# A two-block model on one core: block order of paired products, and the place of GpSimd's subtractions and issues beside them

## Chip, core and metric

The kernel runs on one core of one Trainium2 chip. The metric is the time of one execution on the device in microseconds (us), the median over several runs. Engines: TensorE (PE, with its weight loads PEld), VectorE (DVE), ScalarE (ACT), GpSimd (POOL) and the queue of SyncE (SP).

## What is computed

Two model blocks over 512 positions of width 1024, float32 throughout. The first has two layers: a norm, a wide projection, four kinds of attention (forgetting, top-k, retention, sliding window), gates and merging, an output projection, then a norm and a gated feed-forward of width 2816 with a short convolution. The second (the "tail") adds a modulation, a Fourier and a gated delta mixer, and a feed-forward with a 3x3 convolution. Cut to the lines that the change touches:

```python
for l in range(DEPTH):
    h = rmsnorm(x, attn_norm[l])
    z = h @ w_in[l]                       # tok, kI, qI, kB, q, k, v, gates ...
    ...
    merged = jnp.sum(g * branch, axis=2)
    x = x + merged @ w_out[l]             # "out", 8 products of 128 columns
    h = rmsnorm(x, ffn_norm[l])
    u = causal_dwconv(h @ w_up[l], conv_w[l], conv_b[l])   # "up" f, j
    a, b = jnp.split(u, 2, axis=-1)
    x = x + (jax.nn.silu(a) * b) @ w_down[l]               # "down", 8 products
...
y  = mixer @ w_out                        # tail: "out2"
xl = xl + gt1l * rmsnorm_2(y, g_post_mix) # norm 3
h  = modulate(rmsnorm_2(xl, g_pre_ffn), sh2l, sc2l)        # norm 4, then "up", "down"
```

## The kernel before

**Dense products.** Every projection is cut into products of 128 output columns; a product has 8 blocks (22 for a down product, 4 for a branch), one for each 128 rows of its weights. A block is three matmuls of 128x128 weights over 512 positions (L738 to L740): high part by high part, high by low, low by high, since each operand is held as a rounded part and a rest. Weights come in items of 128x1024 (512 KB, mostly one product), in a fixed stream.

**Where an item goes.** SP loads it into one of 4 raw slots (`load`, L696), as soon as the item four before it has ended on PE (`dense_mark`). GpSimd issues a second copy of it into one of 3 hi slots (`issue(w)`, L2464), which waits until the item three before it has ended. When both have landed, GpSimd subtracts one from the other (`low(w)`, L2474, output `raw_lo`), and PE may open the item (`weights_lo`). GpSimd works in one order written out by hand; an instruction that waits holds all behind it. Its loop over the items of the two layers does `issue(w + 1)`, `low(w)`, then what hangs on item w - 2 (`finished`). Only for `("out", 1)`, and for the second product after a norm, does it take low first.

**Order of the blocks on PE.** `walk` lists the blocks of the products that it is given; for two products it takes a block of each in turn. Such pairs stand where the other operand comes chunk by chunk: tok and kI behind norm (l, 1), up 0,0 and up 0,1 behind norm (l, 2), out 0 and out 1 behind the merging. There PE waits at each k for chunk k's low part, `h_lo`: even chunks from VectorE (L1781, L2105), odd ones from GpSimd (`split_lo_odd`, L2506, and L2532 for the merged sum). Both products of a pair end within a block of each other.

**Norms.** ScalarE squares the 8 chunks, GpSimd adds six times (`add_square`, L2492), PE sums over the rows (`norm_stats`, L860), GpSimd raises to -1/2 (`norm_pow`, L2498), PE spreads the rows (L876), VectorE scales chunk by chunk. ScalarE's square k waits until `square_added` has k - 2 of the sums. Norm X is that of the context (256 positions): its six additions stand behind item `("down", 0)` of layer 1, and PE needs them after product down 0, norm X's rows after product down 1. Norms 3 and 4 lie between out2 and the tail's feed-forward.

**The tail's order on GpSimd** is a straight list: three out2 items ahead, then for products 3 to 7 issue, low and an addition of norm 3; the first two items of up, norm 3, norm 4, `split_lo_odd(4)`; then the loop over up and down. `W_OUT` and `W_UP` are the places of the first out2 and the first up item.

## Time and profile before

| | |
|---|---|
| median of 3 runs | 3184.25 us (3183.17 to 3186.38) |
| the profiled execution | 3182.28 us, its span 3180.5 us |
| TensorE clock granted, mean | 0.973 |
| PE busy | 2976.0 us, 94% of the span, 16704 matmuls |
| GpSimd busy | 1626.1 us, 51% |
| VectorE, ScalarE busy | 1435.0 us, 738.6 us |
| moved by DMA | 491.99 MB, 155 GB/s in the mean |

Times in the trace are microseconds from the span's start. "Idle before" an instruction is the time in which its engine did nothing, and the arrow names what ended it. The granted clock is a share of 2.4 GHz; the clock has two levels, 1.2 and 2.4 GHz. Matmuls overlap, so the pitch from start to start tells what one costs, not its duration.

### The profile page before, as it was taken

Reading aid. Unit: us, or ns where it says so; the run is one execution under the profiler, and the core shown is the slowest. Engines: PE = TensorE matmul, PEld = TensorE weight load, DVE = VectorE, ACT = ScalarE, POOL = GpSimd, SP = SyncE. Lnnn points to the kernel's source line nnn. Section 1 sums busy time; section 2 is a strip of 40 time slices with the busy share of each in tenths; the row PEclk is TensorE's granted clock in tenths of the full one; section 3 lists DMA queues with packets and bytes.
Section 4 is the critical chain, followed back from the end, with each engine's and each line's share of the span. In section 5 each row is a group of like instructions: output and inputs, shape, how many; then the busy total and the mean of one; then the engine's idle time right before and its main releaser. Section 6 shows DMA issues by size and latency. Waiting matters only on the chain.

```text
span 3180.5 us, 41302 instructions
## 1 busy us (share of the span) xinstructions
PE 2976.0 (94%) x16704; PEld 2344.7 (74%) x16704; DVE 1435.0 (45%) x2527; ACT 738.6 (23%) x1585; POOL 1626.1 (51%) x1134
## 2 busy tenths in 40 slices
PE   6999999998999999999999989999899987689998
PEld 4767777777777877677777777777778576578886
DVE  2654443353555027544433525551242377277721
ACT  3334331111121023333322112111132223111110
POOL 5434455556555664344455555545534254456664
PEclk9999999999999999999999999999999999889999
DMA  4433444534666545344444446765433000345554
GB/s 174 168 121 133 146 151 164 174 124 164 231 225 236 187 158 171 130 137 146 141 152 165 153 145 227 248 224 175 169 119 133 14 3 22 99 139 192 192 198 139
DMA packets 133565, 491.99 MB, mean 155 GB/s; under 512 B 14832, under 2 KB 14832, under 8 KB 132608
## 3 DMA queue, kind: packets, MB, share of 16 engines
q1 hardware_dynamic: 70736, 260.86, 25.1%
q0 software_dynamic: 61200, 222.85, 19.5%
q10 hardware_dynamic: 1440, 5.64, 0.5%
q8 instruction: 133, 2.18, 0.3%
q14 instruction: 56, 0.46, 0.1%
HBM read 487.17 MB, written 2.13 MB: 154 GB/s over the span
## 4 chain that ended last, share of the span: by engine, by line
PE 77%; DVE 9%; POOL 6%; issue 5%; DMA 2%; ACT 1%; POOLq 0%; DVEq 0%; ACTq 0%
PE dense L738 21%; PE dense L740 20%; PE dense L739 20%; POOL raw_lo L2474 3%; PE scores L942 2%; PE O L976 2%; PE turned L964 1%; DMA weights_hi<-stream 1%; POOL squares_sum L2492 1%; PE scores L738 1%; PE scores L740 1%; PE scores L739 1%; PE O L1010 1%; DVE row_sum L1957 1%; PE dense L1134 1%
## 5 line engine op out<-in xcount | busy, mean ns | idle before, releaser
L2474 POOL TENSOR_TENSOR raw_lo<-raw,weights_hi 128x1024 fp32r<-128x1024 f32 x425 | 1021.9, 2405 | 101.5 <-DMA weights_hi<-stream 55.8
L738 PE MATMUL dense<-h_hi,weights_hi 128*128 128x512 f32 x2208 | 891.6, 404 | 32.6 <-POOL raw_lo L2474 17.1
L740 PE MATMUL dense<-h_hi,raw_lo 128*128 128x512 f32 x2208 | 868.6, 393 | 0.0
L739 PE MATMUL dense<-h_lo,weights_hi 128*128 128x512 f32 x2208 | 868.2, 393 | 0.0
L2464 POOL DMA_DIRECT2D weights_hi<-stream x425 | 245.0, 576 | 1184.9 <-PE dense L740 1052.2
L738 PEld LDWEIGHTS dense<-h_hi,weights_hi 128*128 128x128 f32 x2208 | 420.0, 190 | 161.5 <-issue 69.3
L740 PEld LDWEIGHTS dense<-h_hi,raw_lo 128*128 128x128 f32 x2208 | 419.1, 190 | 91.3
L739 PEld LDWEIGHTS dense<-h_lo,weights_hi 128*128 128x128 f32 x2208 | 420.3, 190 | 81.3
L738 PE MATMUL dense<-hidden_hi,weights_hi 128*128 128x512 f32 x528 | 207.0, 392 | 6.3 <-POOL raw_lo L2474 6.3
L739 PE MATMUL dense<-hidden_lo,weights_hi 128*128 128x512 f32 x528 | 206.0, 390 | 0.0
L740 PE MATMUL dense<-hidden_hi,raw_lo 128*128 128x512 f32 x528 | 205.9, 390 | 0.0
L2082 DVE SCALAR_TENSOR_TENSOR x<-dense,x 128x512 f32<-128x512 f32 x32 | 22.1, 692 | 304.7 <-PE dense L740 304.7
L2440 DVE SCALAR_TENSOR_TENSOR side_b<-scores,small_sb,side_b 128x441 f32<-128x441 f32 (+2 forms) x176 | 122.4, 695 | 43.5 <-ACT side_b L1740 38.0
L2119 DVE SCALAR_TENSOR_TENSOR side_b<-dense,small_sb,side_b 128x511 f32<-128x511 f32 x88 | 65.9, 749 | 163.5 <-ACT side_b L1581 162.0
L738 PEld LDWEIGHTS dense<-hidden_hi,weights_hi 128*128 128x128 f32 x528 | 99.5, 188 | 28.6 <-POOL raw_lo L2474 7.1
L1393 ACT ACTIVATE swapped<-dense 32x512 f32<-32x512 f32 x168 | 98.9, 589 | 90.7 <-PE dense L740 76.1
L1895 DVE TENSOR_TENSOR y_parts<-O,y_parts 128x512 fp32r<-128x512 f32 x24 | 16.6, 692 | 218.6 <-ACT y_parts L1474 218.6
L740 PEld LDWEIGHTS dense<-hidden_hi,raw_lo 128*128 128x128 f32 x528 | 99.5, 188 | 20.7
L739 PEld LDWEIGHTS dense<-hidden_lo,weights_hi 128*128 128x128 f32 x528 | 99.6, 189 | 20.5
L1966 DVE TENSOR_SCALAR probs<-probs,inv_sum 128x128 f32<-128x128 f32 (+2 forms) x192 | 111.8, 624 | 3.4
L1500 ACT ACTIVATE probs<-probs,neg_max 128x128 f32<-128x128 f32 (+3 forms) x128 | 71.0, 555 | 176.1 <-DVE neg_max L1939 176.1
L1365 ACT ACTIVATE squares<-x 128x512 f32<-128x512 f32 x56 | 34.8, 629 | 316.0 <-DVE x L2082 282.0
(374 smaller groups left out, 4487.3 us busy)
## 6 DMA issues: line engine op xcount, KB each, us to landing
raw<-stream SPq DMA_DIRECT2D x473, 512.0 KB, 3.5
weights_hi<-stream POOLq DMA_DIRECT2D x425, 512.0 KB, 4.6
decays<-stream ACTq DMA_DIRECT2D x8, 512.0 KB, 3.9
gates<-f_scratch SPq DMA_DIRECT2D x2, 1536.0 KB, 8.6
x<-x_in SPq DMA_DIRECT2D x2, 1024.0 KB, 8.2
dft<-dft SPq DMA_DIRECT2D x4, 512.0 KB, 6.7
out<-x SPq DMA_DIRECT2D x4, 512.0 KB, 2.6
const<-consts ACTq DMA_DIRECT2D x1, 1024.0 KB, 10.7
```

The lines of the kernel that those rows point to most:

```text
L738: nc.tensor.matmul(to, wh, xh, start=first, stop=False)
L739: nc.tensor.matmul(to, wh, xl, start=False, stop=False)
L740: return nc.tensor.matmul(to, wl, xh, start=False, stop=final)
L942: last = nc.tensor.matmul(scores[:, hh, 0:n], qT[c % 2][half, s * P:(s + 1) * P], keys[half, k0:k1], start=True, stop=True)
L976: last = nc.tensor.matmul(O[half, m * P:m * P + n], values[:, m, v0:v0 + HEAD_DIM], probT(hh, m, n), start=(m == 0), stop=True, skip_group ...
L1393: last = nc.scalar.activation(swapped[32 * q:32 * q + 32, :], src[32 * (q ^ 1):32 * (q ^ 1) + 32, :], ACT.Copy)
L1500: last = nc.scalar.activation(prob(s, hh, n), src, ACT.Exp, bias=neg_max[:, at:at + 1], scale=QK_SCALE if name == "D" else 1.0, accum_out= ...
L1966: last = nc.vector.tensor_scalar(prob(s, hh, n), prob(s, hh, n), inv_sum[:, at:at + 1], None, ALU.mult)
L2119: nc.vector.scalar_tensor_tensor(out=u, in0=src[:, 0:SEQ - shift], scalar=small[:, at + tap:at + tap + 1], in1=u, op0=ALU.mult, op1=ALU.ad ...
L2440: nc.vector.scalar_tensor_tensor(out=u, in0=v, scalar=small[:, tap:tap + 1], in1=u, op0=ALU.mult, op1=ALU.add).then_inc(conv_step if m < 7 ...
L2464: nc.gpsimd.dma_start(w_hi(s), stream[DENSE.items[DENSE.weight_list[w]]]).then_inc(hi_landed[s], 16)
L2474: nc.gpsimd.tensor_tensor(lo, src, hi, ALU.subtract).then_inc(weights_lo, 1)
```

## The change

Two orders of blocks are added. With `AFTER_NORM` a pair goes in turns through chunks 0 to 3, then the first product takes chunks 4 to 7 and then the second. It holds for tok with kI and for the up pair of the two layers, not for the tail's. With `AFTER_MERGE` out 0 takes chunks 0 to 5, out 1 chunks 0 and 1, out 0 its last two, out 1 the rest. The number of blocks, items and matmuls is the same, and so is the order in which items are opened.

On GpSimd, low(w) comes ahead of issue(w + 1) for `("qI", 0)` and `("up", 1, 0)`, the first items behind such pairs. Norm X's six additions are cut into three behind item down 1 and three behind down 2. In the tail, issue runs one item further ahead of low in out2, the last addition of norm 3 follows low(W_UP), and low(W_UP + 2) comes ahead of issue(W_UP + 3).

```diff
--- before.py
+++ after.py
@@ -129,6 +129,8 @@
 Block = namedtuple("Block", "key k n out item m opens last mark")
 
 
+AFTER_NORM = [(j, k) for k in range(4) for j in range(2)] + [(j, k) for j in range(2) for k in range(4, KC)]
+AFTER_MERGE = ([(0, k) for k in range(6)] + [(1, 0), (1, 1), (0, 6), (0, 7)] + [(1, k) for k in range(2, KC)])
 EARLY = [("ab", 1), ("qkv", 0, 1), ("qkv", 1, 1)]
 
 
@@ -138,26 +140,26 @@
     def __init__(self):
         rows, items, uses = [], [], {}
 
-        def walk(l, *prods):
+        def walk(l, *prods, order=None):
             n = [n_blocks(p) for p in prods]
-            for k in range(max(n)):
-                for p, total in zip(prods, n):
-                    if k < total:
-                        kind = p[0]
-                        if kind == "wb":
-                            item, m = (l, "wb", p[1], p[2] // 2), (p[2] % 2) * PAIRS + k
-                        elif kind == "down":
-                            item, m = (l, "down", (p[1] * FC + k) // KC), (p[1] * FC + k) % KC
-                        elif kind in ("qkv", "ab"):
-                            item, m = (l,) + p[:-1], k
-                        elif kind in ("wf", "pc", "py"):
-                            item, m = None, 0
-                        else:
-                            item, m = (l,) + p, k
-                        rows.append(((l,) + p, k, total, item, m))
+            for j, k in order or [(j, k) for k in range(max(n)) for j in range(len(prods))]:
+                p, total = prods[j], n[j]
+                if k < total:
+                    kind = p[0]
+                    if kind == "wb":
+                        item, m = (l, "wb", p[1], p[2] // 2), (p[2] % 2) * PAIRS + k
+                    elif kind == "down":
+                        item, m = (l, "down", (p[1] * FC + k) // KC), (p[1] * FC + k) % KC
+                    elif kind in ("qkv", "ab"):
+                        item, m = (l,) + p[:-1], k
+                    elif kind in ("wf", "pc", "py"):
+                        item, m = None, 0
+                    else:
+                        item, m = (l,) + p, k
+                    rows.append(((l,) + p, k, total, item, m))
 
         for l in range(DEPTH):
-            walk(l, ("tok",), ("kI",))
+            walk(l, ("tok",), ("kI",), order=AFTER_NORM)
             for p in [("qI", 0), ("qI", 1), ("kB",)] + lead("A", 0):
                 walk(l, p)
             for t in range(NT):
@@ -165,7 +167,7 @@
                     walk(l, p)
             for d in range(KC):
                 walk(l, ("wb", "C", d))
-            walk(l, ("out", 0), ("out", 1))
+            walk(l, ("out", 0), ("out", 1), order=AFTER_MERGE)
             for d in range(2, KC):
                 walk(l, ("out", d))
             self.ffn(walk, l)
@@ -220,7 +222,7 @@
     @staticmethod
     def ffn(walk, l):
         first = int(l == TAIL)
-        walk(l, ("up", 0, first), ("up", 0, 1 - first))
+        walk(l, ("up", 0, first), ("up", 0, 1 - first), order=AFTER_NORM if l < TAIL else None)
         ada = [("ada", q, k) for q in range(ADA_Q) for k in range(KC)] if l < TAIL else []
         for f in range(1, FC):
             for j in (first, 1 - first):
@@ -2565,6 +2567,9 @@
                     norm_pow(name)
                     issue(w + 1)
                     split_lo_odd(name)
+                elif what in (("qI", 0), ("up", 1, 0)):
+                    low(w)
+                    issue(w + 1)
                 else:
                     issue(w + 1)
                     low(w)
@@ -2575,8 +2580,8 @@
                     group_pow(l, PAIRS - 2)
                 if what == ("gate", "C", KC - 1):
                     group_pow(l, PAIRS - 1)
-                if item == (DEPTH - 1, "down", 0):
-                    for step in range(1, KC - 1):
+                if item in ((DEPTH - 1, "down", 1), (DEPTH - 1, "down", 2)):
+                    for step in range(3 * what[1] - 2, 3 * what[1] + 1):
                         add_square("X", step, CTX)
                 if item == (DEPTH - 1, "down", 4):
                     norm_pow("X", CTX)
@@ -2676,14 +2681,14 @@
                 nc.gpsimd.tensor_tensor(y_lo[:, g, :], yT[:, g, :], y_hi_t[:, g, :], ALU.subtract).then_inc(four_lo, 1)
             pool.wait_ge(p_dve, P_MEANS)
             nc.gpsimd.tensor_tensor(oscale[:], osum[:], minus_half[:, 0:TB * GH], ALU.pow).then_inc(l2_ready, 1)
+            issue(W_OUT + 3)
             for d in range(3, KC):
-                issue(W_OUT + d)
+                issue(W_OUT + d + 1)
                 low(W_OUT + d)
                 add_square(3, d - 2)
-            issue(W_UP)
-            add_square(3, KC - 2)
             issue(W_UP + 1)
             low(W_UP)
+            add_square(3, KC - 2)
             norm_pow(3)
             low(W_UP + 1)
             for step in range(1, KC - 1):
@@ -2691,9 +2696,12 @@
             issue(W_UP + 2)
             norm_pow(4)
             split_lo_odd(4)
+            low(W_UP + 2)
+            issue(W_UP + 3)
             for w in range(W_UP + 2, len(DENSE.weight_list)):
-                issue(w + 1)
-                low(w)
+                if w > W_UP + 2:
+                    issue(w + 1)
+                    low(w)
                 what = DENSE.weight_list[w][1:]
                 if what[0] == "up" and what[1] >= 2 and what[2]:
                     hidden_low(what[1] - 2)
```

## Rows read from the trace of the kernel before

**Rows 1.** The page, part 1: each engine's busy time, share of the span, instructions.

```profile
PE 2976.0 (94%) x16704; PEld 2344.7 (74%) x16704; DVE 1435.0 (45%) x2527; ACT 738.6 (23%) x1585; POOL 1626.1 (51%) x1134
```

**Rows 2.** Waits of PE, whole span: us in total, times, longest us.

```profile
PE dense L738 <- POOL raw_lo L2474: 30.6, 11, 6.3
...
PE dense L738 <- issue: 5.3, 2, 2.7
```

**Rows 3.** Windows of PE, out stage, layer 0: us, busy (x), clock, DMA share, GB/s.

```profile
698.37:713.90 15.53, 12.86 (x49) 0.89 0.20 68
716.77:723.90 7.13, 7.13 (x24) 0.76 0.51 190
723.90:729.35 5.45, 5.45 (x26) 1.00 0.60 192
```

**Rows 4.** One line's instructions: L2474 (ns min/median/max), L2464 (landing).

```profile
L2474 POOL TENSOR_TENSOR raw_lo<-raw,weights_hi x425: 463/2402/2912, 28.0 to 3149.9; 128x1024 fp32r<-128x1024 f32 x141, 128x128 fp32r<-128x128 f32 x1
...
DMA to landing us min/median/max: 3.5/4.6/9.4
```

**Rows 5.** Timeline of GpSimd, up pair, layer 0: start us, us, instruction [idle before].

```profile
765.54 1.29 POOL L2506 TENSOR_TENSOR h_lo<-h,h_hi 128x512 fp32r<-128x512 f32 x1 [0.76 <-ACT h_hi L1384]
772.68 0.57 POOL L2464 DMA_DIRECT2D weights_hi<-stream  x1 [5.85 <-PE dense L740]
773.28 2.37 POOL L2474 TENSOR_TENSOR raw_lo<-raw,weights_hi 128x1024 fp32r<-128x1024 f32 x1
...
778.20 2.91 POOL L2474 TENSOR_TENSOR raw_lo<-raw,weights_hi 128x1024 fp32r<-128x1024 f32 x1 [2.04 <-DMA weights_hi<-stream]
```

**Rows 6.** Timeline of PE, end of the same pair and the next item.

```profile
772.22 0.39 PE L738 MATMUL dense<-h_hi,weights_hi 128*128 128x512 f32 x1
...
776.56 0.39 PE L738 MATMUL dense<-h_hi,weights_hi 128*128 128x512 f32 x1
```

**Rows 7.** Timeline of GpSimd, tok and kI, layer 0.

```profile
39.37 1.29 POOL L2506 TENSOR_TENSOR h_lo<-h,h_hi 128x512 fp32r<-128x512 f32 x1 [0.76 <-ACT h_hi L1384]
...
46.67 2.35 POOL L2474 TENSOR_TENSOR raw_lo<-raw,weights_hi 128x1024 fp32r<-128x1024 f32 x1
```

**Rows 8.** Timeline of GpSimd and VectorE, out pair, layer 0.

```profile
699.06 2.81 POOL L2474 TENSOR_TENSOR raw_lo<-raw,weights_hi 128x1024 fp32r<-128x1024 f32 x1
...
703.17 1.27 POOL L2532 TENSOR_TENSOR h_lo<-merged,h_hi 128x512 fp32r<-128x512 f32 x1 [0.80 <-ACT h_hi L1571]
...
714.27 2.36 POOL L2474 TENSOR_TENSOR raw_lo<-raw,weights_hi 128x1024 fp32r<-128x1024 f32 x1
...
702.34 0.68 DVE L2105 TENSOR_TENSOR h_lo<-merged,h_hi 128x512 fp32r<-128x512 f32 x1
```

**Rows 9.** Timeline of GpSimd, squares of norm X and down 1, layer 1.

```profile
2149.79 4.54 POOL L2492 TENSOR_TENSOR squares_sum<-squares_sum,squares 128x256 f32<-128x256 f32 x5 [0.53 <-ACT squares L1365]
...
2154.87 2.35 POOL L2474 TENSOR_TENSOR raw_lo<-raw,weights_hi 128x1024 fp32r<-128x1024 f32 x1
```

**Rows 10.** Windows of PE: down 0, blocks 8 to 11; out2, products 5 to 7.

```profile
2150.86:2161.67 10.81, 4.55 (x13) 0.68 0.49 147
2741.36:2767.12 25.76, 20.33 (x73) 0.87 0.46 143
```

**Rows 11.** Timeline of GpSimd, out2, product 5.

```profile
2736.53 0.58 POOL L2464 DMA_DIRECT2D weights_hi<-stream  x1
2741.55 2.33 POOL L2474 TENSOR_TENSOR raw_lo<-raw,weights_hi 128x1024 fp32r<-128x1024 f32 x1 [4.44 <-DMA weights_hi<-stream]
```

**Rows 12.** Timeline of GpSimd, up pair of the tail.

```profile
2807.38 1.29 POOL L2506 TENSOR_TENSOR h_lo<-h,h_hi 128x512 fp32r<-128x512 f32 x1 [1.55 <-ACT h_hi L1384]
2810.70 0.61 POOL L2464 DMA_DIRECT2D weights_hi<-stream  x1 [2.04 <-PE scores L740]
2811.34 2.36 POOL L2474 TENSOR_TENSOR raw_lo<-raw,weights_hi 128x1024 fp32r<-128x1024 f32 x1
...
2816.55 2.39 POOL L2474 TENSOR_TENSOR raw_lo<-raw,weights_hi 128x1024 fp32r<-128x1024 f32 x1 [2.36 <-DMA weights_hi<-stream]
```

## The prediction

> **What bounds the kernel now.** The page comes first: TensorE is busy 94% of the span [rows 1]. So the question is never whether GpSimd or the queues are busy (POOL stands at 51%), only where TensorE stands still. The list of PE's waits answers it: the dense products waited 30.6 us, 11 times, for GpSimd's subtraction that makes `raw_lo` of a weight item, and 5.3 us in two gaps that the profile calls "issue" [rows 2]. In the timeline all of these but two short ones lie at places that the diff touches. A window of steady work gives the yardstick: one item (8 blocks of three matmuls) takes PE 5.45 us at full clock, 0.68 us a block [rows 3]. Beside it an item costs GpSimd 0.57 us to issue and about 2.40 us to subtract; a transfer issued by GpSimd lands 3.5 to 9.4 us later, 4.6 at the median [rows 4]. With three hi slots, an item's transfer can start only when the item three before it has ended.
>
> **The pairs after a norm (tok with kI, up 0 with up 1, two layers each).** In the up pair of layer 0 GpSimd ends its last `h_lo` at 766.83, then sits 5.85 us in front of issue(up 1,1), which waits for the first of the pair; both end within one block of each other, at about 772.4 and 773.1. Only then comes low(up 1,0), 773.28 to 775.65 [rows 5]. PE's last block of the pair starts at 772.22 and the second block of the next item at 776.56: 4.34 us for two blocks that need 1.36, so 2.98 us lost [rows 6]. The same subtraction after tok and kI starts at 46.67 [rows 7], again right behind an issue, and costs 2.96 by the same reckoning.
>
> After the change low goes first. It can run from 766.85 to 769.2, under the pair's last blocks; its gap goes whole. The price to look for is chunks: order AFTER_NORM wants chunk 7 at block 11 of the pair and not at 14. Blocks 0 to 7 are unchanged, so block 11 starts at about 769.5, and the last `h_lo` ends at 766.83 [rows 5]: 2.6 us to spare, no cost. In tok and kI block 11 stands at 42.9 against 40.66 [rows 7].
>
> What is next late is low of the item after that. Its transfer can be issued 2.04 us (three blocks) earlier, at about 770.64, since the first product ends three blocks earlier. In the old run it took from 772.68 to 778.20 with two raw loads beside it, 5.5 us, and its subtraction 2.91 [rows 5]. With one raw load beside it at first, the median 4.6 [rows 4] is nearer. PE wants that item at 772.9 + 5.45 = 778.35. By 4.6 and 2.4 us it is ready at 777.6: no wait. By 5.5 and 2.9 it is ready at 779.05: 0.7 us of wait. So between 0 and 0.7 us a site; I take 0.2, nearer to the quiet case. Four sites: 2 x 2.96 + 2 x 2.98 - 0.8 = **11.1 us**.
>
> The Trainium skill (DMA: Bandwidth & Descriptors, Anatomy of one DMA) fits a GpSimd-issued transfer by 2.0 us plus its bytes at 436 GB/s: by estimate 3.2 us for 512 KB alone, 4.4 with one of the same size beside it, 5.6 with two. The trace agrees (3.5 least, 4.6 median, 5.5 here), and by that page the wait would be nearer to none.
>
> **The out pair.** Here two gaps go. The window from out 0's first block to the pair's end takes 15.53 us, 16 blocks need 10.90: 4.63 lost [rows 3], of which 2.67 is PE in front of out 1's first block until low(out 1) ends at 701.87 [rows 8], the rest the clock, granted at 0.89 over the window (its levels are 1.2 and 2.4 GHz). From 713.90 to 716.77 PE stands behind low(out 2), 714.27 to 716.63, which again sits behind an issue [rows 8]: 2.87. The item then takes 7.13 instead of 5.45, at a clock of 0.76: 1.68 [rows 3]. Together 9.18; layer 1 repeats it with 9.21.
>
> With AFTER_MERGE out 1's first block comes sixth, at 698.37 + 6 x 0.68 = 702.45, when `raw_lo` is ready (701.87). Chunk 6 is wanted at 703.8; VectorE writes it until 703.02. Chunk 7 is wanted at 704.5 and GpSimd ends it at 704.44 [rows 8]: no margin, so I charge 0.1 us. Out 0 then ends at 705.2, issue(out 3) and low(out 2) follow at 705.7 and 706.3 to 708.7, and the pair ends at 709.3. PE never stops, and so I expect the clock to stay at 2.4 GHz: both falls followed a gap of 2.7 us. Gain 18.4 - 0.2 = **18.2 us**.
>
> **The squares of norm X.** Behind low(down 0) GpSimd adds six squares, the last five from 2149.79 to 2154.33, and only then issues and makes low(down 1), 2154.87 to 2157.22 [rows 9]. PE wanted it at 2150.86; by the window the next four blocks took until 2161.67, 10.81 us for 2.72, at 0.68 of the clock [rows 10]: 8.1 lost. After the change low(down 1) comes first, ready at about 2148.1; three additions end at 2151.7, low(down 2) runs to 2154.7 (wanted at 2156.3), three more additions end near 2157.4. PE needs the whole sum at the end of product down 0, 2160.4: 3 us to spare. Gain **8.1 us**.
>
> **out2 in the tail.** The loop issues an item and subtracts it at once, so the landing is never hidden: issue at 2736.53, `raw_lo` from 2741.55 [rows 11]. GpSimd's round is then some 8 us against PE's 5.45, and PE, one item after another, loses its lead. From the start of product 5 to the end of product 7 it takes 25.76 us at 0.87 of the clock, where three items need 16.35 [rows 10]: 9.4 lost. With issue(d + 1) in front of low(d), transfer and subtraction of an item have two items of PE's time (10.9 us) for 0.6 + 4.6 + 2.4. The first of them, low(3), moves behind a wait for product 1 (until 2725.5) and ends at 2728.5, wanted at 2730.5. Square 6 of norm 3 is now added behind low of the next stage, at 2757.0; PE wants the sum at 2757.7. Cover 0.7 us; without it each us is lost whole. Gain **9.4 us**.
>
> **The tail's up pair.** Block order is unchanged there. low(W_UP + 2) can start at 2808.66 instead of 2811.34 [rows 12], so the 2.76 us gap before that item nearly closes. But the item after it is issued behind this subtraction at 2811.1, not at 2810.70; it landed 5.85 us later, and its subtraction ended at 2818.95, just when PE wanted it [rows 12]. So PE starts it no sooner: the gap moves one item on. Now four transfers start within 1.3 us instead of three, so it may land 0 to 1.2 us later again; with the 0.4 of the issue that is 0.1 to 1.6 us lost, and 0.6 is what I take. No gain here: **0.6 us slower**. By the page's fit, four 512 KB transfers at once would take 6.8 us, and the loss would be 1.3.
>
> **The sum.** 11.1 + 18.2 + 8.1 + 9.4 - 0.6 = 46.2 us. About 13 of them are clock. The profiled execution took 3182.28 us (span 3180.5) and would take 3136.1; the median of the runs shown lies 1.97 above it, so 3184.25 - 46.2 = 3138.0. PE hands time gained in one stage to the next: the other stages start from PE's own products, and its other waits (norms, VectorE's top-k, the scan) lie after them in order.
>
> **Rivals.**
> (a) The gap moves instead of going. What I find in the tail happens also at the four pairs after norms, because the transfer of the second next item is late. For it: a wait of 2.04 us for its landing in rows 5. Against: it starts 2 us earlier now. Nothing of the 11.1 would be left: 3149. Chance 0.12.
> (b) The merge order bites, or the clock. Chunk 7 has no margin; a late `h_lo` of 1.3 us and a fall of the clock (1.7) in both layers cost 6 us; a few new falls elsewhere cost the same. 3145. Chance 0.12.
> (c) Slower. Moving low in front of issue leaves GpSimd one transfer behind, and the backlog does not heal. Each such item costs what out2 shows, (25.76 - 16.35) / 3 = 3.1 us; from 15 such items on the gain is eaten, and 30 give 3184 - 46 + 93 = 3231. Against: a round of GpSimd's is 3.0 to 4.3 us against 5.45, so it gains over 1 us an item. Chance 0.03.
> (d) The change doesn't do what it says: the subtractions were waiting for something else, their landing for instance, and the same end is kept. 3184. Against: no low at these places shows such a wait but the second one. Chance 0.03.
> More gain than in my forecast (fewer clock falls elsewhere, 3130) has 0.04; the forecast, 3132 to 3144, has 0.66.
>
> A measurement of this kernel can tell some 0.2% (6.4 us) from no change. Faster by more: 0.66 + 0.12 + 0.12 + 0.04 = 0.94; same 0.03; slower 0.03. The range of 8 in 10 takes in (a) and (b) and their ends: 3129 to 3153.
>
> **What would show it.** Right: PE's wait for `raw_lo` on the dense lines falls from 30.6 to under 6 us; the 2.7 us gaps after tok/kI, out, up are gone; the clock stays full over the out pairs; out2 runs at 5.45 us an item. In the tail the gap of 2.8 us stands one item later. Wrong: waits for DMA in front of low of the second next item over 0.7 us at the pairs, new waits for `h_lo` at blocks 8 to 11, or a wait of norm 3's sum at PE.

## The result, and the profile of the changed kernel

The changed kernel took 3138.98 us (median of 4 runs, 3135.69 to 3141.66) beside 3184.68 us for the kernel before on the same chip: ratio 0.9857, 95% interval 0.9844 to 0.9869. That is 45.7 us less, where 46.2 had been forecast. Measured once more with the last experiments it took 3136.56 us against 3186.22 (ratio 0.9852, 0.9836 to 0.9869). The profiled execution took 3141.11 us with a span of 3139.3, so 41.2 us less than the span before. Line numbers of the kernel have moved by two: L738 is now L740, L2464 is L2466, L2474 is L2476.

The page's part 1, beside [rows 1]: TensorE's busy time fell by 12 us, since less of it runs at 1.2 GHz; the rest of the gain is time in which it no longer stands.

```profile
PE 2963.7 (94%) x16704; PEld 2338.8 (75%) x16704; DVE 1448.9 (46%) x2527; ACT 738.4 (24%) x1585; POOL 1625.7 (52%) x1134
```

The waits of PE over the whole span (us in total, times, longest us), beside [rows 2]: the wait of the dense line for `raw_lo` fell from 30.6 us in 11 places to 8.2 in 3, and the row "issue" of 5.3 us is gone. The tail's gap of 2.8 us isn't in the 30.6: before the change it stood in a row of its own, the second below, since that product writes to another tile.

```profile
PE dense L740 <- POOL raw_lo L2476: 8.2, 3, 3.5
...
PE scores L738 <- POOL raw_lo L2474: 2.8, 1, 2.8
```

The windows of PE in the changed kernel (us, busy, matmuls, clock, DMA share, GB/s) answer to [rows 3] and [rows 10]. In order: the out pair of layer 0, the product behind it, blocks 3 to 11 of down 0 in layer 1, and out2 from the last block of product 4 to that of product 7. Busy time equals the window in each, and the clock is full.

```profile
695.63:706.66 11.03, 11.03 (x49) 1.00 0.57 183
706.66:712.10 5.44, 5.44 (x25) 1.00 0.59 206
2118.31:2124.57 6.26, 6.26 (x29) 1.00 0.73 255
2705.44:2721.76 16.32, 16.32 (x73) 1.00 0.57 194
```

GpSimd's timeline of the up pair in layer 0 (start, duration, instruction, idle time before it), beside [rows 5]: the subtraction of up 1,0 now stands directly behind the last `h_lo`, the two issues come 2.7 us apart as the two products end, and the subtraction of up 1,1 ends at 765.47. PE wanted it at 765.5.

```profile
752.82 1.30 POOL L2508 TENSOR_TENSOR h_lo<-h,h_hi 128x512 fp32r<-128x512 f32 x1 [0.76 <-ACT h_hi L1386]
754.08 2.40 POOL L2476 TENSOR_TENSOR raw_lo<-raw,weights_hi 128x1024 fp32r<-128x1024 f32 x1
757.75 0.57 POOL L2466 DMA_DIRECT2D weights_hi<-stream  x1 [1.28 <-PE dense L742]
760.47 0.53 POOL L2466 DMA_DIRECT2D weights_hi<-stream  x1 [2.15 <-PE dense L742]
762.56 2.91 POOL L2476 TENSOR_TENSOR raw_lo<-raw,weights_hi 128x1024 fp32r<-128x1024 f32 x1 [1.56 <-DMA weights_hi<-stream]
```

The same for the out pair of layer 0, beside [rows 8]: `raw_lo` of out 1 is ready at 699.16 and wanted at 699.7; the `h_lo` of chunk 7 ends at 701.75, where PE wants it at 701.85; the subtraction of out 2 ends at 706.04, 0.6 us ahead of its product.

```profile
696.32 2.84 POOL L2476 TENSOR_TENSOR raw_lo<-raw,weights_hi 128x1024 fp32r<-128x1024 f32 x1
...
700.47 1.28 POOL L2534 TENSOR_TENSOR h_lo<-merged,h_hi 128x512 fp32r<-128x512 f32 x1 [0.79 <-ACT h_hi L1573]
703.05 0.57 POOL L2466 DMA_DIRECT2D weights_hi<-stream  x1 [1.30 <-PE dense L742]
703.64 2.40 POOL L2476 TENSOR_TENSOR raw_lo<-raw,weights_hi 128x1024 fp32r<-128x1024 f32 x1
```

In the tail's up pair, beside [rows 12], both issues follow the first subtraction as one entry (x2), and the transfer of the first of them landed at 2772.94, 6.73 us after its issue.

```profile
2763.52 2.40 POOL L2476 TENSOR_TENSOR raw_lo<-raw,weights_hi 128x1024 fp32r<-128x1024 f32 x1
2766.21 1.21 POOL L2466 DMA_DIRECT2D weights_hi<-stream  x2 [0.29 <-PE scores L742]
2773.08 2.33 POOL L2476 TENSOR_TENSOR raw_lo<-raw,weights_hi 128x1024 fp32r<-128x1024 f32 x1 [5.66 <-DMA weights_hi<-stream]
```

To see where the 41.2 us of the span came from, the start of the last block of every product was compared in the two traces; a step in that difference belongs to the place where it occurs.

| place | forecast us | step in the traces us |
|---|---|---|
| four pairs after norms | 11.1 | 2.97 + 2.94 + 3.00 + 2.85 = 11.8 |
| out pair, two layers | 18.2 | 9.13 + 8.89 = 18.0 |
| squares of norm X | 8.1 | 8.1 |
| out2 | 9.4 | 9.4 |
| tail's up pair | -0.6 | -2.6 |
| three norms ahead of pairs, clock | none | +3.3 |
| turn A 3, layer 1 | none | -3.5 |
| qkv 2 in the tail | none | -2.9 |
| all the rest | none | -0.4 |

The parts named in the forecast give 44.7 us of the 46.2. Below it stand gains and losses at places that the change doesn't touch, and the experiments show that these come and go from one kernel to the next.

### The profile page after: what moved, and what is told of

Its sections match the earlier page's. It is cut to its first block, busy times and chain, and to the rows that moved or that the text cites. A ratio compares the mean times of both kernels' runs of the same rounds, so it can differ in the third digit from the quotient of the medians.

```text
span 3139.3 us, 41302 instructions
## 1 busy us (share of the span) xinstructions
PE 2963.7 (94%) x16704; PEld 2338.8 (75%) x16704; DVE 1448.9 (46%) x2527; ACT 738.4 (24%) x1585; POOL 1625.7 (52%) x1134
## 4 chain that ended last, share of the span: by engine, by line
PE 82%; DVE 7%; POOL 5%; issue 3%; DMA 2%; ACT 1%; POOLq 0%; DVEq 0%; ACTq 0%
PE dense L740 22%; PE dense L742 21%; PE dense L741 21%; POOL raw_lo L2476 2%; PE scores L944 2%; PE O L978 2%; PE turned L966 1%; POOL squares_sum L2494 1%; PE scores L740 1%; PE scores L741 1%; PE scores L742 1%; DMA weights_hi<-stream 1%; PE O L1012 1%; DVE row_sum L1959 1%; PE dense L1136 1%
## 5 line engine op out<-in xcount | busy, mean ns | idle before, releaser
L2476 POOL TENSOR_TENSOR raw_lo<-raw,weights_hi 128x1024 fp32r<-128x1024 f32 x425 | 1021.9, 2405 | 81.6 <-DMA raw<-stream 38.9
L740 PE MATMUL dense<-h_hi,weights_hi 128*128 128x512 f32 x2208 | 890.3, 403 | 14.8 <-DVE h_lo L1783 10.2
L2466 POOL DMA_DIRECT2D weights_hi<-stream x425 | 244.8, 576 | 1169.1 <-PE dense L742 1058.6
L740 PEld LDWEIGHTS dense<-h_hi,weights_hi 128*128 128x128 f32 x2208 | 418.8, 190 | 141.7 <-issue 55.4
L740 PE MATMUL dense<-hidden_hi,weights_hi 128*128 128x512 f32 x528 | 206.2, 390 | 0.0
L740 PEld LDWEIGHTS dense<-hidden_hi,weights_hi 128*128 128x128 f32 x528 | 99.1, 188 | 21.6 <-issue 0.9
L740 PE MATMUL dense<-y_parts,weights_hi 128*128 128x512 f32 x256 | 103.5, 404 | 2.8 <-DVE y_parts L2008 2.8
## 6 DMA issues: line engine op xcount, KB each, us to landing
const<-consts ACTq DMA_DIRECT2D x1, 1024.0 KB, 10.8
```

The lines of the kernel that those rows point to most:

```text
L740: nc.tensor.matmul(to, wh, xh, start=first, stop=False)
L2466: nc.gpsimd.dma_start(w_hi(s), stream[DENSE.items[DENSE.weight_list[w]]]).then_inc(hi_landed[s], 16)
L2476: nc.gpsimd.tensor_tensor(lo, src, hi, ALU.subtract).then_inc(weights_lo, 1)
```

## The experiments

All ratios are against the kernel before, run on the same chip between them. "Stretch" is the time in the profiled execution from the first block of a place to the last block that its gaps can reach.

### The out order alone, whole and half

```
+AFTER_MERGE = ([(0, k) for k in range(6)] + [(1, 0), (1, 1), (0, 6), (0, 7)] + [(1, k) for k in range(2, KC)])
-            walk(l, ("out", 0), ("out", 1))
+            walk(l, ("out", 0), ("out", 1), order=AFTER_MERGE)
```

> The kernel before with one part of the change: the block order AFTER_MERGE for the out pair of both layers. Theory: both gaps of the pair are the place of the first product's end and of the second product's first block, so the order alone brings 9.1 us a layer, as in the kernel after: 18.3 us in all, 3166 us, and the trace shows neither the 2.7 us wait in front of out 1's first block nor the 2.8 us wait in front of out 2. Rival: the pair waits for GpSimd's h_lo of chunk 7 (no margin) or the time comes back in the up stage: 3172 us or more. Rival: nothing but the whole change together works: 3184 us.

Measured: 3164.29 us against 3184.18, ratio 0.9939 (0.9917 to 0.9962), so 19.4 us less (12 to 26). The stretch from out 0's first block to out 3's fell from 25.53 us (both windows of [rows 3] and the gap between them) to 16.48, by 9.05 us, in layer 1 from 25.56 to 16.55. No GpSimd line was edited: the end of the first product alone moves the issue and the subtraction behind it.

For the half, the second line of the order reads:

```
+AFTER_MERGE = ([(0, k) for k in range(6)] + [(1, k) for k in range(6)] + [(0, 6), (1, 6), (0, 7), (1, 7)])
```

> The kernel before with half of AFTER_MERGE: out 1 opens sixth, but out 0 ends at block 14 and out 1 at block 15, as before. Theory: the first gap goes (2.67 us and the clock fall behind it, 4.6 us a layer), the second one in front of out 2 stays, with its own fall of the clock (2.87 + 1.68 us a layer): 9.2 us gained, 3175 us. Rival A: the clock fell for another reason than the gap, so the first half gives only 2 x 2.67 = 5.3 us: 3179 us. Rival B: the time not lost in the first gap is lost in the second, which ends at the same moment: 3184 us.

Measured: ratio 0.9966 (0.9953 to 0.9980), 10.8 us less (6 to 15). The windows of the same stretch in this kernel, layers 0 and 1:

```profile
695.95:715.33 19.38, 16.66 (x73) 1.00 0.48 162
1812.87:1833.90 21.03, 18.30 (x74) 0.92 0.45 151
```

In both, span less busy is 2.7 us: the second gap stands as before. Rival B falls, the two gaps are independent; rival A's 5.3 us lies outside the interval too, narrowly. But the clock fell behind the remaining gap in layer 1 and not in layer 0, with the same gap and the same work. So the clock's part, priced at 3.6 us a layer, is not a fixed price of the gaps.

### TensorE kept at work in the gaps

```
                         if e.item[0] < TAIL and e.item[1:] in (("out", 1), ("out", 2)):
                             pe.wait_ge(t_copied, T_LAYER * (e.item[0] + 1))
                             for _ in range(11):
                                 nc.tensor.matmul(turned[:, 0, :], h_hi_t[:, 0, 0:P], h_hi_t[:, 0, :], start=True,
                                                  stop=True, skip_group_check=True)
                         pe.wait_ge(weights_lo, DENSE.weights[e.item] + 1)
```

> The kernel before, where TensorE works in the two gaps of each out pair: 11 matmuls of 128x512 into a bank that nobody reads, ahead of the wait for raw_lo of out 1 and of out 2 (some 2.4 of the 2.7 and 2.9 us). The waits stay as long as they are. Theory: the clock falls behind a gap because PE stood still; with the gaps filled it stays at 2.4 GHz over the out pairs, and 1.96 + 1.68 us a layer come back, 7.3 us: 3177 us. Rival: the clock falls at this place whether PE stands still or not: 3184 us. Rival: the filling matmuls end after raw_lo is ready and delay the product by more than the clock gives back: over 3184 us.

Measured: ratio 0.9989 (0.9978 to 1.0000), 3.5 us less (0 to 7). The windows of the stretch, layers 0 and 1, have the clock at 1.00:

```profile
700.96:724.20 23.24, 22.12 (x96) 1.00 0.39 135
1819.91:1843.10 23.19, 22.06 (x95) 1.00 0.40 137
```

The clock stayed full in all four filled gaps, and 2.3 and 2.4 us of 25.5 came back, where 3.6 had been forecast. Most of the missing part is the filling itself: out 1 opened at 705.53, 1.0 us after its `raw_lo` was ready at 704.50. How much this shows is limited by the kernels that leave the gaps empty. There are ten such stretches (the kernel before and the four experiments that don't touch the out order, two layers each), and three of them kept the clock too, at 22.3 us:

```profile
1826.34:1848.65 22.31, 16.91 (x74) 1.00 0.40 142
```

(the experiment with out2 alone, layer 1). By these a kept clock is worth 3.2 us a layer and not 3.6. The other seven stretches lie at 23.6 to 26.8 us with a clock of 0.81 to 0.93. Counted by single gaps, those of the halved pair included, a fall stood behind 13 of 22 empty gaps and behind none of the four filled ones. So an empty gap of 2.7 us made a fall of the clock likely at this place and not certain. That standing still is the cause is supported by the two filled stretches and by every stretch without a gap at 1.00; it isn't proved by two.

### The norm order alone, and GpSimd's order alone

```
+AFTER_NORM = [(j, k) for k in range(4) for j in range(2)] + [(j, k) for j in range(2) for k in range(4, KC)]
-            walk(l, ("tok",), ("kI",))
+            walk(l, ("tok",), ("kI",), order=AFTER_NORM)
-        walk(l, ("up", 0, first), ("up", 0, 1 - first))
+        walk(l, ("up", 0, first), ("up", 0, 1 - first), order=AFTER_NORM if l < TAIL else None)
```

> The kernel before with the block order AFTER_NORM in tok with kI and up 0 with up 1 of both layers; GpSimd's order of issue and low is as before. Theory: the first product ends 3 blocks (2.04 us) earlier, issue and the low behind it go with it, and the gap of 2.97 us in front of the next item shrinks to about 0.9 us at each of the four places: 8.2 us gained, 3176 us. Rival: the gap is set by the landing, which does not come earlier: 3184 us.

Measured: ratio 0.9971 (0.9958 to 0.9984), 9.2 us less (5 to 13). The steps at the four places are 1.99, 2.02, 2.04 and 2.05 us, as the three blocks (2.04 us) of the theory.

The other half leaves the block order and puts low first:

```
+                elif what in (("qI", 0), ("up", 1, 0)):
+                    low(w)
+                    issue(w + 1)
```

> The kernel before with only GpSimd's order changed at the items behind the pairs after norms: low first, then issue; the block order is as before. Theory: the gap in front of the next item goes at all four places, but the item after it is issued at the old time while TensorE wants it 2.97 us earlier, so a gap of 2.5 to 2.9 us stands one item later, as in the tail of the kernel after: 0 to 1.9 us gained, and up to 3 us lost where its transfer is slow, 3182 to 3187 us. Rival: the landing has reserve, and moving low alone brings the whole 11.9 us: 3172 us.

Measured: ratio 0.9999 (0.9988 to 1.0010): nothing. The rival, 11.9 us, lies outside. GpSimd's timeline of the up pair in layer 0 shows why:

```profile
769.28 1.21 POOL L2464 DMA_DIRECT2D weights_hi<-stream  x2 [3.60 <-PE dense L740]
776.83 2.34 POOL L2474 TENSOR_TENSOR raw_lo<-raw,weights_hi 128x1024 fp32r<-128x1024 f32 x1 [6.34 <-DMA weights_hi<-stream]
```

Both products end within one block, both issues go out together behind them, and the first transfer lands after 7.41 us (6.61 and 5.58 us behind tok and kI of layers 0 and 1, 5.52 behind up of layer 1). PE stands 2.07 us in front of up 1,1 and 2.83 in front of qI 1 (0.62 and 1.82 in layer 1). That is rival (a) of the prediction, to be seen wherever only half of the change is made. There is a second wait that neither theory had, in PE's list of waits:

```profile
PE dense L738 <- DVE side_a L2119: 3.7, 2, 1.9
```

Up 1,0 writes into the bank of up 0,0, and VectorE still reads that bank with its convolution until 771.4. In the kernel before this wait lay hidden under the wait for `raw_lo`; in the changed kernel the first product ends three blocks earlier and the bank is free in time (this row of PE's is in neither of the two traces). So AFTER_NORM serves two ends, the slot for the next transfer and the bank, and GpSimd's order is worth something only with it: 8.1 of the 11.8 us come with the block order, and the remaining 3.7 with both.

### The squares of norm X alone, out2 alone

```
-                if item == (DEPTH - 1, "down", 0):
-                    for step in range(1, KC - 1):
+                if item in ((DEPTH - 1, "down", 1), (DEPTH - 1, "down", 2)):
+                    for step in range(3 * what[1] - 2, 3 * what[1] + 1):
```

> The kernel before with only the squares of norm X moved: three behind low(down 1), three behind low(down 2). Theory: PE's 2.1 us-and-clock loss at product down 0 goes whole, 8.0 us of PE's time between the last up block and the end of down 0, and nothing comes back since the sum is needed 3 us after its end: 3176 us. Rival: the additions now delay low(down 3) or the norm, and half comes back: 3180 us.

Measured: ratio 0.9973 (0.9963 to 0.9984), 8.6 us less (5 to 12); the step at down 0 is 8.11 us. The window from its first block to block 12 was 16.39 us at a clock of 0.79 before, and is now

```profile
2144.74:2153.03 8.29, 8.29 (x40) 1.00 0.72 253
```

For out2, the loop of the tail as in the change, without the part for the up pair:

```
+            issue(W_OUT + 3)
             for d in range(3, KC):
-                issue(W_OUT + d)
+                issue(W_OUT + d + 1)
                 low(W_OUT + d)
                 add_square(3, d - 2)
-            issue(W_UP)
-            add_square(3, KC - 2)
             issue(W_UP + 1)
             low(W_UP)
+            add_square(3, KC - 2)
             norm_pow(3)
```

> The kernel before with only the loop of out2 changed: each item issued one round ahead, the last square of norm 3 behind low of the up stage. Theory: products 5 to 7 run at 5.45 us each instead of 25.76 us for the three, 9.4 us gained, 3175 us, and the tail's up pair stays as before with its gap of 2.8 us. Rival: the late square holds the norm at PE (0.7 us of cover) and takes back 1 to 3 us: 3177 us.

Measured: ratio 0.9973 (0.9960 to 0.9986), 8.6 us less (4 to 13). From the start of product 5 to the last block of product 7 it was 22.41 us at 0.85, and is now

```profile
2745.40:2761.04 15.64, 15.64 (x71) 1.00 0.57 202
```

The whole step in the traces is 9.4 us, and no wait for the sum of norm 3 took it back. Added up, the parts measured alone (19.4, 9.2 and 0.3 for the two halves of the norm pairs, 8.6, 8.6) give 46.1 us; the whole, in two measurements, 45.7 and 49.7. Each part is known to some 4 to 7 us only, so this sum tells that no large part is missing, and the steps in the traces tell the parts.

### The tail's up pair undone

```
-            low(W_UP + 2)
-            issue(W_UP + 3)
             for w in range(W_UP + 2, len(DENSE.weight_list)):
-                if w > W_UP + 2:
-                    issue(w + 1)
-                    low(w)
+                issue(w + 1)
+                low(w)
```

> The changed kernel with GpSimd's order in the tail's up pair as it was before: issue(W_UP + 3), then low(W_UP + 2). Theory: the change only moved the gap one item on and made the transfer slower, so undoing it brings a gap of 2.8 us in front of up 1,1, none in front of up 1,0, and 2.0 to 2.6 us less in all: 3136.5 us against 3139. Rival: the transfer of up 1,0 takes 6.7 us for another reason, the gap of 3.5 us stays and that of 2.8 us comes on top: 3142 us.

Beside it ran the changed kernel once more:

> The changed kernel as it is, beside the three that follow. All theories: 3139 us, with VectorE's negation of row_max taking 2.7 to 2.9 us in the last turn of branch A (0.17 us elsewhere) in one or both layers.

Measured: 3136.81 us against 3136.56 for the changed kernel beside it (ratios 0.9850 and 0.9852, intervals of 0.003): the two can't be told apart by their times, and the 2.0 to 2.6 us forecast are not seen there. (In the changed kernel's second profile the negation took 2.85 and 2.91 us, held in both layers.) The traces can. From the first block of the pair to the last of up 1,0 it took 26.31 us in the kernel before, 29.31 and 29.01 in the two profiles of the changed kernel, 27.45 with this part undone. GpSimd in this kernel:

```profile
2762.47 0.61 POOL L2466 DMA_DIRECT2D weights_hi<-stream  x1 [1.50 <-PE scores L742]
2763.11 2.36 POOL L2476 TENSOR_TENSOR raw_lo<-raw,weights_hi 128x1024 fp32r<-128x1024 f32 x1
2765.41 0.57 POOL L2466 DMA_DIRECT2D weights_hi<-stream  x1
2769.70 2.81 POOL L2476 TENSOR_TENSOR raw_lo<-raw,weights_hi 128x1024 fp32r<-128x1024 f32 x1 [3.72 <-DMA weights_hi<-stream]
```

The gap of 2.76 us is back in front of up 1,1, and there is none in front of up 1,0, so the gap does move by one item, and the undone order is 1.6 to 1.9 us better in the traces. Over all profiles with the block order of before in this pair, the nine with the old order lie at 25.87 to 28.22 us and the three with the new one at 29.01 to 29.31. But the transfer of up 1,0 took 7.08 us here, more than in the changed kernel (6.73). My reason for its slowness, four transfers in 1.3 us, isn't borne out: with the old order it took 5.3 to 7.1 us over nine profiles, with the new one 6.3 to 6.7 over three. The Trainium skill (DMA: Bandwidth & Descriptors, Anatomy of one DMA), by whose fit four transfers at once would take an estimated 6.8 us, is met by 6.73, 6.30 and 6.57 here and not by the 7.08 with three. What the new order takes away is the cover: the old one waits 2.8 us first, and a transfer of 7.1 us ends within that.

### The negated maximum in turn A 3

The loss of 3.5 us in the attention of layer 1 lies at a place that the change doesn't touch. VectorE negates `row_max` there, 128x2 numbers, while GpSimd has just issued a transfer and starts to subtract the weights of q B 1. The changed kernel, VectorE first:

```profile
1321.75 2.75 DVE L1941 TENSOR_SCALAR neg_max<-row_max 128x2 f32<-128x2 f32 x1
...
1322.06 2.41 POOL L2476 TENSOR_TENSOR raw_lo<-raw,weights_hi 128x1024 fp32r<-128x1024 f32 x1
```

and the kernel before:

```profile
1341.01 0.17 DVE L1939 TENSOR_SCALAR neg_max<-row_max 128x2 f32<-128x2 f32 x1
...
1341.55 2.41 POOL L2474 TENSOR_TENSOR raw_lo<-raw,weights_hi 128x1024 fp32r<-128x1024 f32 x1
```

The negation ends at 1324.50 and the subtraction at 1324.46: the short instruction was held for the whole of the long one. ScalarE's exponentials wait for it, and PE's next transposes stood 2.88 us instead of 0.68, with a fall of the clock behind them. Over the eleven profiles without an edit at this place there are 22 cases (two layers each). In all eleven in which the subtraction began 0.31 to 0.48 us after the negation, that took 2.75 to 2.94 us; in all eleven in which it began 0.54 us or more after, 0.17. In layer 0 the kernel before was held (2.94 us) and so was the changed one, in layer 1 only the changed one. So a shift of a quarter of a microsecond in what came before decides over some 3.7 us.

The Trainium skill (SBUF — State Buffer, Who interferes with whom) names the mechanism: VectorE and GpSimd share a pair of ports, the one that starts first has it for its whole instruction and the other is blocked, and a `tensor_scalar` from SBUF to SBUF can be of the kind that takes it. The trace agrees in the end time. By the trace's start times, though, the negation began ahead of the subtraction, which the page would not expect to lose. It did not begin ahead of all of GpSimd's work: directly before the subtraction stands the issue of a transfer, 0.60 us long.

```profile
1321.43 0.60 POOL L2466 DMA_DIRECT2D weights_hi<-stream  x1 [8.86 <-PE dense L742]
```

In all eleven held cases the negation began 0.13 to 0.32 us after that issue had begun, in the other eleven at most 0.07 us after it or before it. Whether the issue takes part in the holding, or the subtraction holds before its recorded start, isn't shown.

```
                 else:
                     issue(w + 1)
+                    if what == ("q", "B", 1):
+                        pool.wait_ge(negmax_ready, t_use(l, 3, 3) + 1)
                     low(w)
```

> The changed kernel, in which GpSimd waits for the negated maximum of turn A 3, last part, before it subtracts the weights of q B 1, in both layers. So that subtraction can no longer run beside the negation. In the runs so far the negation took 2.75 to 2.94 us in the eight cases in which the subtraction began 0.30 to 0.48 us after it, and 0.17 us in the ten in which it began 0.54 us or more after it. Theory: the subtraction holds VectorE's instruction; with the wait it takes 0.17 us in both layers, PE's gap behind it is 0.7 us and not 2.9, and with the clock 3.6 us a layer come back: 3132 us where both layers are hit, as in the changed kernel's trace. Rival: the long negation has another cause, and nothing changes: 3139 us. Rival: the wait moves the collision to the next instruction of VectorE: 3139 us as well, with another instruction over 2 us.

Measured: 3135.67 us (ratio 0.9849, 0.9826 to 0.9872) against 3136.56 for the changed kernel: no difference that can be told, where 7 us less had been forecast for a kernel that is held in both layers. In the trace the negation takes 0.17 us in both layers, none of the 64 is longer, and the steps at turn A 3 against the changed kernel's first trace are 3.75 and 3.77 us:

```profile
L1941 DVE TENSOR_SCALAR neg_max<-row_max x64: 168/169/172, 92.2 to 1445.9; 128x2 f32<-128x2 f32 x64
```

But the subtraction began 1.68 and 0.54 us after the negation, outside the band in which it is held even without the wait. So this run alone doesn't tell the wait from luck, and if executions of the changed kernel miss the band about half of the time, as the eleven profiles do, the median moves by less than the profile.

### A version with what was learned

The wait above, GpSimd's order of before in the tail, and a block order with chunk 7 of the first product at block 12 for two pairs:

```
+LATE_CHUNKS = ([(j, k) for k in range(4) for j in range(2)]
+               + [(0, 4), (0, 5), (1, 4), (0, 6), (0, 7), (1, 5), (1, 6), (1, 7)])
-        walk(TAIL, ("ab", 0), ("qkv", 0, 0))
+        walk(TAIL, ("ab", 0), ("qkv", 0, 0), order=LATE_CHUNKS)
-        walk(l, ("up", 0, first), ("up", 0, 1 - first), order=AFTER_NORM if l < TAIL else None)
+        walk(l, ("up", 0, first), ("up", 0, 1 - first), order=AFTER_NORM if l < TAIL else LATE_CHUNKS)
```

> The changed kernel with the wait of the run before it, GpSimd's order in the tail as before the change, and a block order for the tail's up pair and for ab with qkv 0 in which chunk 7 of the first product comes at block 12 and not at 14. Theory: the wait brings 7.1 us; the tail's order 2.6 us, and 1.4 us more since the first product ends 1.36 us earlier (a gap of 1.2 to 1.4 us in front of up 1,1 for 2.8); the gap in front of qkv 2 falls from 3.5 to about 2.1 us: 12.5 us in all, 3126.5 us. Rival: chunk 7 or 6 is not ready at its block, and the pairs win nothing: 3130 us.

Measured: 3126.55 us (3125.27 to 3128.82), ratio 0.9822 (0.9806 to 0.9837), 10.0 us below the changed kernel measured beside it (3134.43 to 3138.76). The forecast of 12.5 us less had been taken from 3139; that 3126.5 was met is luck in part, since the changed kernel itself came out at 3136.56. The tail's stretch is 25.64 us against 29.31: GpSimd's timeline there has

```profile
2753.90 0.61 POOL L2468 DMA_DIRECT2D weights_hi<-stream  x1 [1.33 <-PE scores L744]
2754.54 2.38 POOL L2478 TENSOR_TENSOR raw_lo<-raw,weights_hi 128x1024 fp32r<-128x1024 f32 x1
2756.86 0.57 POOL L2468 DMA_DIRECT2D weights_hi<-stream  x1
2758.35 2.39 POOL L2478 TENSOR_TENSOR raw_lo<-raw,weights_hi 128x1024 fp32r<-128x1024 f32 x1 [0.92 <-DMA weights_hi<-stream]
```

so that the gap in front of up 1,1 is 1.43 us and none follows. The gap in front of qkv 2 is 0.80 us (3.51 and 2.33 in the profiles of the changed kernel). Chunk 7 made PE wait 0.2 to 0.3 us at its block, little beside the 1.36 us won.

> The best version once more, for its time and for two more cases of the negation beside the subtraction. With the wait in place the subtraction began 0.54 us or more after the negation in three of four cases so far, where it is not held without the wait either; only one case (0.45 us, 0.17 us long) lay in the band in which all eleven cases without the wait were held. Theory: the negation takes 0.17 us again wherever the subtraction begins, and the time is 3126.5 us. Rival: in the band of 0.30 to 0.48 us it is held for 2.7 us or more in spite of the wait; then the one case was luck and the time is up to 7 us longer.

Measured: 3128.07 us (3127.90 to 3130.99) against 3181.48, ratio 0.9830 (0.9817 to 0.9844). The negation took 0.17 us in both layers again, with the subtraction 1.76 and 0.60 us behind it. Over the three profiles with the wait that is six cases of 0.17 us, one of them inside the band: in e_best, layer 0, the negation began at 219.00 and the subtraction at 219.45, and it wasn't held. Eleven of eleven without the wait were. This speaks for the wait as a cure and rests on one case. In that case the negation began 0.15 us after GpSimd's issue, so the issue alone doesn't hold it.

## Why the prediction was right, point by point

**Where TensorE stood still.** The list of waits named the places, and they carried the whole gain: 44.7 us by the steps in the traces, of 46.2 forecast. The sign that I gave, a wait for `raw_lo` under 6 us, was missed in the first profile (8.2) and met in the second (5.8). Both consist of the tail's gap, which the 30.6 of before did not hold, and of that in front of qkv 2; the first has 1.1 us in front of up 7,1 of layer 0 beside them (0.8 before). The gap in front of qkv 2 follows a transfer that took 7.02 us in the first and 5.81 in the second, and between 5.2 and 7.9 us over all kernels with its order unchanged.

**Pairs after norms, 11.1 against 11.8.** The step that I left between 0 and 0.7 us a site, the second next item, cost 0.1 us at most: its transfers took 4.45, 4.67, 4.88 and 4.79 us, so the median of [rows 4] was the right row and not the 5.5 of [rows 5]. At up in layer 0 it was ready with no reserve, since its subtraction took 2.91 us. Rival (a) is real, but only without the block order, as GpSimd's order alone showed. Chunks 4 to 7 came in time. One sign of being wrong was badly chosen: a wait for DMA of over 0.7 us in front of that item's low stood at all four sites (1.34 to 1.76 us, 1.56 in the timeline above), and PE lost nothing by it, since what counts is when the low ends against when PE wants it.

**Out pair, 18.2 against 18.0.** Both gaps went, the clock stayed full. The margin of chunk 7 was 0.1 us, as read from [rows 8], and cost nothing: the first half of rival (b), a late `h_lo`, didn't occur. What was mis-stated is how sure the clock's share was. The kernel before had it in both layers of its profile, and so the sum took 7.3 us for it (2 x 3.64); in ten stretches with the gaps three show none. An average execution gains some 2 us less here than the profiled one. At tok with kI it is the other way: the profile of before shows no fall behind the gap in front of qI 0, and the sum took none, but in the five other kernels that leave this gap a fall followed in six of ten cases, and cost 1.4 to 1.6 us in five of them and 2.8 in one. Both are errors of reading one execution as the rule, and in the total they happen to work against each other.

**Squares of X and out2, 8.1 and 9.4 against 8.1 and 9.4.** Both held when done alone. The cover of 0.7 us over norm 3's last square was enough.

**The tail, -0.6 against -2.6.** The mechanism was right: no gap in front of up 1,1, one of 3.53 us in front of up 1,0. The term mis-sized is what follows the gap. Counted from the last block of the first product, up 1,0 started 10.50 us later and 9.82 before: 0.7 us, near the 0.6 that I had taken (1.5 in the other two profiles with this order, 11.28). But its eight blocks then took 6.46 us from first to last, for 4.76 before, since the clock fell behind the new gap, where it had not fallen behind the old one of 2.76: 1.7 us that the sum had left out. It counted the clock where a gap went and forgot it where a gap came. Over all profiles a fall followed the new gap of 3.5 us in three of three and the old one of 2.76 in three of nine.

**Rivals (c) and (d)** are ruled out by the time and by the traces: no backlog of GpSimd's showed, and each part but GpSimd's order behind the norm pairs gained alone what it had been priced at. Of rival (b) the second half, new falls of the clock elsewhere, did occur: the profile has them at turn A 3 and in the tail.

**What the sum didn't hold.** Gains and losses at untouched places were as large as its smaller terms: 3.5 us at turn A 3, 2.9 at qkv 2, 3.3 of clock at the norms. They cancelled to about 3 us, and that the total came within 0.5 us of the forecast is luck to that extent. The range of 3129 to 3153 had been drawn from the rivals, not from these; it would have held with the gain alone or the losses alone (some 3133 and 3142 us).

## What to carry to other kernels

Where two products share a stage and the next weights wait for the slot of the first, let the first end early: that alone moves the issue, the subtraction and the bank, while moving only the subtraction ahead of the issue moves the gap one item on and uncovers whatever it hid. When a gap is moved, look for what it covered (a bank, a slow transfer) and charge the clock at its new place as well. Read how often the clock falls there from several profiles, not from one. And read a change's parts from steps in the trace, since a short instruction held by a neighbour's long one can swing 3.7 us on a shift that has nothing to do with the edit.

## What the runs showed of the hardware that was not expected

A negation of 128x2 numbers on VectorE took 2.75 to 2.94 us instead of 0.17 when GpSimd's subtraction of 128x1024 began 0.31 to 0.48 us after it (11 of 22 cases), and 0.17 from 0.54 us on. Why an instruction that by the record starts first and needs 0.17 us is still held isn't settled.

The same transfer of 512 KB, issued at the same place of the program, took 5.17 to 7.88 us in front of qkv 2 (12 profiles) and 5.32 to 7.08 us in the tail's up pair (9 profiles with the old order). The number of transfers that start beside it doesn't order the latter: 7.08 us came with the order that starts fewer at once. In the last version, where the next raw load starts 1.4 us later, it took 4.30 and 4.59 us in the up pair. What went along with the long ones is the transfer that GpSimd issued next, 2.93 us later. While the first was under way, GpSimd's queue (packets, MB, share of the 16 engines) moved this in the kernel with the tail undone (window 2762.47 to 2769.56, 7.08 us) and in that with the squares of X alone (2802.91 to 2808.23, 5.32 us):

```profile
q0 software_dynamic: 274, 1.00, 39.4%
...
q0 software_dynamic: 182, 0.68, 34.3%
```

The transfer itself is 0.52 MB of it. So in the slow case nearly all of the later transfer had moved before the earlier one landed, in the quick one about a third. Which of the two is the cause isn't shown.

A gap of 2.7 us of TensorE is followed by a fall of its clock at some places and hardly at others. Over all profiles there are 55 gaps of 2.66 to 2.77 us at five places, all entered at full clock, and 23 of them were followed by 1.2 GHz: in front of out 1 6 of 10, of out 2 7 of 12, of qI 0 6 of 12, of the tail's up 1,1 3 of 9, and of up 1,0 in the two layers 1 of 12. What sets the places apart was not tried.
